# A weight ring of seven 1 MB pairs in place of thirteen 512 KB tiles, in a two-block transformer kernel

## The chip, the core and the metric

The kernel runs on one core of one Trainium2 chip. The metric is the device time of one launch in microseconds. A core has a matrix engine (TensorE, in the profile PE, with its weight load as PEld), three engines for elementwise work (VectorE as DVE, ScalarE as ACT, GpSimd as POOL), a queueing engine (SyncE, as SP) and 16 DMA engines that all queues share. SP issues the weight transfers, POOL the gathers, and ACT a few small transfers. Everything is float32.

## The reference, cut to what matters

Two transformer blocks are run on 256 tokens of width 1024. The first has two attentions and a layer that looks up 16 experts for each of 8 heads and each token; the second has a spatial mixer, an attention over blocks and a dense layer of width 4096.

```python
def first_block(x, c, ...):
    mod = silu(c) @ w_ada + b_ada                      # 6 vectors of 1024
    h = modulate(rms_norm(x, g_mix), sh1, sc1)
    proj = h @ w_in                                    # q, k, v of both attentions, two gates
    o_sb, o_d = stick_breaking_attention(...), dilated_attention(...)
    merged = sigmoid(gate_sb) * (o_sb @ w_sb_o) + sigmoid(gate_d) * (o_d @ w_dil_o)
    x = x + gt1 * (merged @ w_out)
    h2 = modulate(rms_norm(x, g_ffn), sh2, sc2)
    return rms_norm(x + gt2 * peer_ffn(h2, w_pq, peer_keys, peer_u, peer_v), g_final)

def peer_ffn(h, ...):                                  # per token: 8 heads x 16 experts
    q = h @ w_pq
    expert, gate = top 16 of the sums of two top 16 lists of q against peer_keys
    act = gelu(h . peer_u[expert])
    return sum(gate * act * peer_v[expert])            # u and v rows: 2 x 1024 numbers each

def second_block(x, p, ...):
    u, v, q, k, v_att, g_a, g_b = split(rms_norm(x) @ w_in_2)
    x = x + (sigmoid(g_a) * sgu_mixer(u, v) + sigmoid(g_b) * moba_attention(q, k, v_att)) @ w_out_2
    x = x + square(relu(rms_norm(x) @ w_ff1_2)) @ w_ff2_2
    x = x + sigmoid(rms_norm(x) @ w_ple_gate_2) * (p @ w_ple_proj_2)
    return rms_norm(x)
```

## The kernel before, in words

**Tiles and stages.** The 256 tokens are two tiles of 128. First come the projections of the first block (w_in, in part for both tiles), then the branches and the output projection of tile 0. From then on the expert rows of tile 0 are gathered (128 turns; the names call one head of one tile a unit u, so u is 0 to 15, and each unit has 16 turns k), while TensorE does the attentions, gates, branches and output of tile 1 beside them (`beside`). Then the rows of tile 1 are gathered (128 more turns) while TensorE runs the whole second block of tile 0. Last, the second block of tile 1 runs with no gathers beside it.

**A gather turn.** POOL issues one indirect DMA (L1289) that brings 128 rows of 8 KB, 1 MB, into a row slot. There are nine row slots of 1 MB: three of their own, two in the buffers `tmp` and `merged` (only for the first 62 rows), and four that are the ring's slots 0 to 7, two each. VectorE takes the dot products (L2181), ScalarE and VectorE make the weight (L1417, L2201, L2209), ScalarE writes a diagonal matrix into `dg` (L1425, sixteen in turn) and TensorE multiplies it with the second half of the row (L757 to L760, `accumulate`), two turns behind. The last of these counts `v_used`, which frees the row slot for POOL and the diagonal for ScalarE.

**Weights.** All weights but w_ada come in tiles of 512 KB, 4 KB in each of 128 partitions (384 KB for the branches), in the order of the list FIRST. The tile names: sq, sk, sv, dq, dk, dv are the projections of the two attentions, ga and gb the gates, br0 and out0 the branches and output of tile 0 (lsv, ldv, lga, lgb, br1, out1 those of tile 1), q0 to q15 the query weights of the 16 units in two halves, w0 and w1 the 138 tiles of the second block for tile 0 and tile 1. SP goes through FIRST in order (`first_tiles`, L1206). Each tile waits until TensorE has used what was in its slot. The ring has 13 slots: 12 in rotation at first; while the row slots hold slots 0 to 7, only 5; near the end of the gathers the eight come back. Six tiles of tile 1 (`GUESTS`) go early into the unused row slots. The modulation weights w_ada come first in 512 KB blocks on SP (L1224) and then as eight 2 MB transfers on POOL's queue (L1271), two buffers in turn, each freed by the dot products L1918 on VectorE.

**Turns and weights together.** During the second block of tile 0, one step is one weight tile (`quarter`, L968, four matmuls of 128x512) and one gather turn. The two halves of a unit's query (`query`, L718) run in turns 5 and 7 of every 16; in FIRST they stand two to three tiles apart. The wait of a tile on TensorE is in `tile`:

```python
slot, landed = SLOT[name]
pe.wait_ge(tile_in[slot], landed)
```

## Time and profile before

| | |
|---|---|
| time, median of 3 runs | 1377.2 us (1374.71 to 1377.25) |
| the profiled execution: time, span of its trace | 1375.88 us, 1374.1 us |
| TensorE busy, VectorE busy | 1199.9 us, 735.0 us |
| ScalarE busy, GpSimd busy | 334.5 us, 304.4 us |
| DMA traffic | 517.51 MB, 106557 packets, mean 377 GB/s |
| GpSimd's queue (gathers, large part of w_ada) | 285.23 MB, 51.0% of 16 engines' span |
| SyncE's queue | 227.25 MB, 43.6% |
| chain of work that ended last | TensorE 54%, DMA 32%, VectorE 8%, ScalarE 3% |

All times in the trace count from the start of its span. "A <- B" in a view means that A writes from B, and in the waits that A waited for B. A matmul group of the page shows modelled ends, so a busy TensorE is not one at its peak. PEclk is the granted share of TensorE's clock. The DMA share of a stretch can read slightly over 1, since packets overlap; at 1.00 to 1.03 the DMA engines have no gap. Packets of a row of a gather are 8 KB, packets of a weight tile 4 KB, and each transfer adds 16 packets of a few bytes.

### The profile page before, as it was taken

To read this page: it belongs to the slowest core of one execution; us is meant where nothing else is said; L and a number is where in the kernel's file an instruction comes from. 1 tells how busy PE (TensorE), PEld (TensorE's weight loads), DVE (VectorE), ACT (ScalarE), POOL (GpSimd) and SP (SyncE) were. 2 spreads that over 40 slices of the span, in tenths; PEclk is the share of its full clock that TensorE was granted. 3 is DMA by queue.
4 is the path that set the end of the run, shared out by engine and by line. 5 is a ranking of instruction groups with operands and counts; after the bars stand their busy time and mean duration, and the time that the engine had idled before them with its cause. 6 is when DMAs were issued, how large, how long until landed. Compare 5 with 4: busy or idle time off the path is not lost.

```text
span 1374.1 us, 17081 instructions
## 1 busy us (share of the span) xinstructions
PE 1199.9 (87%) x6004; PEld 615.1 (45%) x6004; DVE 735.0 (53%) x2087; ACT 334.5 (24%) x914; POOL 304.4 (22%) x271
## 2 busy tenths in 40 slices
PE   5999998978867866779898989899877999999998
PEld 4788975535534531223333333333222344544444
DVE  6456467967776776886556565554644332310002
ACT  2412134222211231333222211211110243311102
POOL 0000013434333343343232322222233100000000
PEclk9999999989898998789999999999999999999999
DMA  9999989999999999999999999999999899778882
GB/s 370 405 363 395 384 328 370 419 419 418 417 417 418 412 407 419 409 367 415 416 417 416 415 412 416 401 417 411 417 417 417 313 411 363 224 265 285 291 302 87
DMA packets 106557, 517.51 MB, mean 377 GB/s; under 512 B 12133, under 2 KB 12901, under 8 KB 73194
## 3 DMA queue, kind: packets, MB, share of 16 engines
q0 software_dynamic: 41088, 285.23, 51.0%
q1 hardware_dynamic: 63364, 227.25, 43.6%
q10 hardware_dynamic: 2022, 3.95, 0.8%
q8 instruction: 49, 0.80, 0.2%
q14 instruction: 34, 0.28, 0.1%
HBM read 513.76 MB, written 1.05 MB: 375 GB/s over the span
## 4 chain that ended last, share of the span: by engine, by line
PE 54%; DMA 32%; DVE 8%; ACT 3%; issue 2%; SPq 1%; POOL 0%; ACTq 0%; DVEq 0%
PE ps_M L968 28%; DMA ring<-in_w_second 15%; DMA ring<-in_peer_uv,arena 12%; PE ps_T L757 8%; PE ps_M L489 3%; DMA ring<-in_w_pq 2%; DMA arena<-in_w_ada 2%; PE ps_M L512 2%; PE ps_M L659 2%; DVE ring L2181 2%; PE ps_M L682 2%; PE ps_OT L956 1%; PE ps_M L718 1%; DVE arena L2181 1%; DVE arena L1918 1%
## 5 line engine op out<-in xcount | busy, mean ns | idle before, releaser
L968 PE MATMUL ps_M<-ring,arena 128*128 128x512 f32 x1072 | 499.0, 604 | 36.2 <-DMA ring<-in_w_second 35.3
L968 PEld LDWEIGHTS ps_M<-ring,arena 128*128 128x128 f32 x1072 | 190.7, 190 | 300.2 <-issue 242.3
L1289 POOL DMA_INDIRECT ring<-in_peer_uv,arena x137 | 160.3, 1170 | 336.0 <-PE ps_T L760 317.9
L757 PE MATMUL ps_T<-ring,arena 64*64 64x512 f32 x274 | 159.5, 671 | 58.0 <-ACT arena L1425 58.0
L1289 POOL DMA_INDIRECT arena<-in_peer_uv,arena x105 | 121.4, 1156 | 234.6 <-PE ps_T L760 221.1
L758 PE MATMUL ps_T<-ring,arena 64*64 64x512 f32 x274 | 159.5, 671 | 0.0
L759 PE MATMUL ps_T<-ring,arena 64*64 64x512 f32 x274 | 159.5, 671 | 0.0
L760 PE MATMUL ps_T<-ring,arena 64*64 64x512 f32 x274 | 159.5, 671 | 0.0
L757 PE MATMUL ps_T<-arena 64*64 64x512 f32 x210 | 115.7, 635 | 22.1 <-ACT arena L1425 22.0
L1417 ACT ACTIVATE arena<-arena 128x2 f32<-128x2 f32 x128 | 25.8, 201 | 393.3 <-DVE arena L2201 389.9
L2181 DVE SCALAR_TENSOR_TENSOR ring<-ring,merged 128x1024 f32<-128x1024 f32 x73 | 88.8, 1220 | 53.1 <-DMA ring<-in_peer_uv,arena 52.8
L760 PE MATMUL ps_T<-arena 64*64 64x512 f32 x210 | 115.8, 635 | 0.0
L759 PE MATMUL ps_T<-arena 64*64 64x512 f32 x210 | 115.8, 635 | 0.0
L758 PE MATMUL ps_T<-arena 64*64 64x512 f32 x210 | 115.7, 635 | 0.0
L2181 DVE SCALAR_TENSOR_TENSOR ring<-ring,arena 128x1024 f32<-128x1024 f32 x64 | 77.9, 1220 | 35.2 <-DMA ring<-in_peer_uv,arena 32.7
L757 PEld LDWEIGHTS ps_T<-ring,arena 64*64 64x64 f32 x274 | 29.3, 141 | 142.9 <-ACT arena L1425 92.3
L2181 DVE SCALAR_TENSOR_TENSOR arena<-arena,merged 128x1024 f32<-128x1024 f32 x55 | 67.1, 1222 | 34.7 <-DMA arena<-in_peer_uv,arena 34.7
L1425 ACT ACTIVATE arena<-ident,arena 128x64 f32<-128x64 f32 x256 | 80.8, 340 | 19.8 <-DVE arena L2209 16.9
L2181 DVE SCALAR_TENSOR_TENSOR arena<-arena 128x1024 f32<-128x1024 f32 x50 | 60.8, 1220 | 19.7 <-DMA arena<-in_peer_uv,arena 16.1
L659 PEld LDWEIGHTS ps_M<-hT,ring 128*128 128x128 f32 x512 | 62.9, 203 | 13.2 <-issue 13.1
L659 PE MATMUL ps_M<-hT,ring 128*128 128x128 f32 x512 | 66.4, 290 | 0.0
L2209 DVE SCALAR_TENSOR_TENSOR arena<-arena 128x2 f32<-128x2 f32 x128 | 20.5, 160 | 79.1 <-ACT arena L1417 77.4
(349 smaller groups left out, 1727.3 us busy)
## 6 DMA issues: line engine op xcount, KB each, us to landing
ring<-in_w_second SPq DMA_DIRECT2D x274, 512.0 KB, 4.7
ring<-in_w_in SPq DMA_DIRECT2D x66, 512.0 KB, 13.1
arena<-in_w_ada POOLq DMA_DIRECT2D x8, 2048.0 KB, 16.2
ring<-in_w_pq SPq DMA_DIRECT2D x28, 512.0 KB, 5.3
arena<-in_w_ada SPq DMA_DIRECT2D x16, 512.0 KB, 15.1
ring<-in_w_out SPq DMA_DIRECT2D x16, 512.0 KB, 5.5
ring<-in_w_br SPq DMA_DIRECT2D x16, 384.0 KB, 9.4
ring<-in_peer_uv,arena POOLq DMA_INDIRECT x137
```

Of the source, the lines that this page charges most:

```text
L489: m = mm(bank[:, 0:T], w[:, c, :], hT[:, c, :], start=c == 0, stop=c == KC - 1)
L512: m = mm(bank[:, 0:n * P], hT[:, c, tile_tok(tt)], slots(lo, n)[:, :, c, :], start=c == 0, stop=c == KC - 1)
L659: m = mm(bank[:, 0:P], w[:, c, :], hT[:, c, tile_tok(t)], start=c == 0, stop=c == KC - 1)
L682: m = mm(bank[:, 0:P], w[:, c, :], tile_merged[:, c, :], start=c == 0, stop=c == KC - 1)
L757: mm(ps["T0"][low, :], d[low, :], row[low, 0:512], start=first, stop=last)
L758: mm(ps["T1"][low, :], d[high, :], row[high, 512:1024], start=first, stop=last)
L759: top = mm(ps["T0"][high, :], d[low, :], row[low, 512:1024], start=first, stop=last)
L760: bottom = mm(ps["T1"][high, :], d[high, :], row[high, 0:512], start=first, stop=last)
L968: m = mm(bank, left[c], w[:, c, :], start=first and c == 0, stop=last and c == 1)
L1289: pool.indirect_dma_start(row_slots[s], None, A["peer_uv"], bass.IndirectOffsetOnAxis(ap=expert[:, u % 3, k:k + 1], axis=0))\
L1425: F(dg[:, n % 16, :], twice, ACT.Copy, scale=wgt[:, u % 2, k:k + 1]).then_inc(diag_ready, 1)
L2181: V.scalar_tensor_tensor(up_row(n), up_row(n), 1.0, h_rows[u // NH], ALU.mult, ALU.mult, accum_out=act_x[:, u % 2, k:k + 1]).then_inc(dott ...
```

## The change

The ring has 14 slots and is handled as seven pairs. Two neighbours in FIRST are one transfer of 1 MB (8 KB in each partition; 6 KB for two branch tiles), with one semaphore and one wait for a free pair. `in_pairs` lays the weights out so on the host. The number of bytes is the same. In the opening all 14 slots rotate. While rows hold slots 0 to 7, three pairs rotate in place of five tiles. The nine row slots stay as they were.

The extra 4 KB per partition is taken from the arena: `dg` has 8 diagonals in place of 16 (ScalarE waits for `v_used` of 8 turns back, not 16), half of the table `rel0` moves into `tmp`, `expert_f` and `act_t` share room with `pos_f` and `act_b`.

FIRST is rearranged where two neighbours were not neighbours before: the halves of a query stand together. TensorE's instructions and their order are the same. SP has 203 fewer transfers and one more (rel0 comes in two).

```diff
-RING, OPENING = 13, 12
+RING = 14
-ARENA = 28272
-SECOND_END = 18254
+ARENA = 27248
+SECOND_END = 17792
+DIAGONALS = 8
...
     if phase in (3, 4):
-        FIRST += [(what, c) for c in range(3)] + [(f"q{u}", 0), (what, 3), (f"q{u}", 1)] + [(what, c) for c in range(4, KC)]
+        FIRST += [(what, c) for c in range(4)] + [(f"q{u}", 0), (f"q{u}", 1)] + [(what, c) for c in range(4, KC)]
...
-for n in range(LEAD + QUARTERS):
+for n in range(0, LEAD + QUARTERS, 2):
+    turns_here = [t for t in TURN_AT[n:n + 2] if t is not None]
+    for t in turns_here:
+        if t // TOPK + NH + 2 < NU and t % TOPK == 5:
+            FIRST += [(f"q{t // TOPK + NH + 2}", half) for half in (0, 1)]
     if n >= LEAD:
-        FIRST.append(("w0", n - LEAD))
-    if TURN_AT[n] is not None:
-        if TURNS // TOPK + NH + 2 < NU and TURNS % TOPK in (5, 7):
-            FIRST.append((f"q{TURNS // TOPK + NH + 2}", TURNS % TOPK // 7))
+        FIRST += [("w0", n - LEAD), ("w0", n - LEAD + 1)]
...
-order = list(range(OPENING))
-for n, name in enumerate(FIRST):
+order = list(range(PAIRS))
+for n in range(0, len(FIRST), 2):
+    pair = FIRST[n:n + 2]
     if n == SHARED:
-        order = [RING - 1] + list(range(VR, RING - 1))
+        order = [6, 4, 5]
...
-        rel0 = carve(AH, P)
+        rel0 = tmp[:, 4:8, :].rearrange("p a (h k) -> p (a h) k", k=P), carve(AH // 2, P)
...
             def tile(name):
                 slot, landed = SLOT[name]
-                pe.wait_ge(tile_in[slot], landed)
+                pe.wait_ge(tile_in[slot // 2], landed)
...
-                for name in FIRST[lo:hi]:
+                for name in FIRST[lo:hi:2]:
...
-                    to = slots(slot, 1).rearrange("p s c n -> p (s c n)")[:, 0:n]
-                    eng.dma_start(to, src).then_inc(tile_in[slot], 16)
+                    to = slots(slot, 2).rearrange("p s c n -> p (s c n)")[:, 0:n]
+                    eng.dma_start(to, src).then_inc(tile_in[slot // 2], 16)
...
-                if n >= 16:
-                    act.wait_ge(v_used, n - 15)
-                F(dg[:, n % 16, :], twice, ACT.Copy, scale=wgt[:, u % 2, k:k + 1]).then_inc(diag_ready, 1)
+                if n >= DIAGONALS:
+                    act.wait_ge(v_used, n - DIAGONALS + 1)
+                F(dg[:, n % DIAGONALS, :], twice, ACT.Copy, scale=wgt[:, u % 2, k:k + 1]).then_inc(diag_ready, 1)
...
+def in_pairs(tiles, order=None):
+
+
+    tiles = tiles[list(range(len(tiles))) if order is None else order]
+    return tiles.reshape(len(tiles) // 2, 2, P, -1).transpose(0, 2, 1, 3).reshape(len(tiles) // 2, P, -1)
```

Two places of SP's order are shown. SP's queue where the gathers begin, before: after the output tiles of tile 0 (in_w_out) come q0 (in_w_pq), the guests (to the arena), lsv and the first gates of tile 1 (in_w_in), and q2 (in_w_pq) with the next three gates. M0 and M1 are the PSUM banks whose finished product frees the slot.

```order
L1206 DMA ring<-in_w_pq 128x1024 [waits done_M1]
L1206 DMA arena<-in_w_in 128x1024 [waits ada_used] x4
L1206 DMA arena<-in_w_pq 128x1024 [waits ada_used] x2
L1206 DMA ring<-in_w_in 128x1024 [waits done_M0]
L1206 DMA ring<-in_w_in 128x1024 [waits done_M1]
L1206 DMA ring<-in_w_in 128x1024 [waits done_M0]
L1206 DMA ring<-in_w_in 128x1024 [waits done_M1]
L1206 DMA ring<-in_w_in 128x1024 [waits done_M0]
L1206 DMA ring<-in_w_in 128x1024 [waits done_M1]
L1206 DMA ring<-in_w_pq 128x1024
L1206 DMA ring<-in_w_pq 128x1024 [waits done_M0]
L1206 DMA ring<-in_w_in 128x1024 [waits done_M1]
```

The same place of SP's queue in the change: the row after q2 is the pair (lga1, lgb1).

```order
L1216 DMA ring<-in_w_pq 128x2048 [waits done_M1]
L1216 DMA arena<-in_w_in 128x2048 [waits ada_used] x2
L1216 DMA arena<-in_w_pq 128x2048 [waits ada_used]
L1216 DMA ring<-in_w_in 128x2048 [waits done_M1] x3
L1216 DMA ring<-in_w_pq 128x2048 [waits done_M1]
L1216 DMA ring<-in_w_in 128x2048 [waits done_M1]
L1216 DMA ring<-in_w_in 128x2048 [waits done_M0]
```

What moved: before, the three tiles lga1, lgb1 and lga2 waited only for output tiles of tile 0 (slots 9 to 11). Now pair 4, where lga1 and lgb1 go, holds lsv0 and lsv1 and is free only after TensorE's `values(("lsvA", 1))`, and lga2 and lgb2 wait for `values(("lsvB", 1))`.

SP's queue at unit 11 of the second block's weights, before: w_pq is q11, SA the bank of the queries.

```order
L1206 DMA ring<-in_w_second 128x1024 [waits done_M0]
L1206 DMA ring<-in_w_second 128x1024 [waits w_used] x2
L1206 DMA ring<-in_w_pq 128x1024 [waits w_used]
L1206 DMA ring<-in_w_second 128x1024 [waits done_M1]
L1206 DMA ring<-in_w_second 128x1024 [waits w_used]
L1206 DMA ring<-in_w_pq 128x1024 [waits w_used]
L1206 DMA ring<-in_w_second 128x1024 [waits w_used]
L1206 DMA ring<-in_w_second 128x1024 [waits done_SA]
```

The same place in the change:

```order
L1216 DMA ring<-in_w_second 128x2048 [waits done_M0]
L1216 DMA ring<-in_w_pq 128x2048 [waits w_used]
L1216 DMA ring<-in_w_second 128x2048 [waits done_M1]
L1216 DMA ring<-in_w_second 128x2048 [waits w_used]
L1216 DMA ring<-in_w_second 128x2048 [waits done_SA]
L1216 DMA ring<-in_w_second 128x2048 [waits done_M0]
```

What moved: q11 stands as one pair ahead of w0 14 and 15, and the pair w0 18 and 19 waits for the second half of the query (`done_SA`, turn 7); before, the tile that followed the first half's slot was w0 18 as well, but it waited for the first half alone (turn 5). All SP transfers behind it wait in the same queue. This recurs at units 12 to 15.

## Rows read from the trace of the kernel before

**Rows 1.** busy us of PE, PEld, DVE, ACT, POOL, then PEclk, DMA share, GB/s

```profile
34.00:172.00 138.00, 135.94 (x849) 117.10 (x848) 75.34 (x152) 36.54 (x77) 6.18 (x8) 1.00 1.02 387
...
206.00:240.00 34.00, 29.42 (x211) 18.70 (x213) 24.94 (x74) 14.54 (x33) 13.78 (x12) 1.00 0.97 370
240.00:578.00 338.00, 259.96 (x1762) 140.76 (x1754) 249.57 (x772) 82.36 (x283) 128.82 (x111) 0.89 1.01 416
...
612.00:1068.00 456.00, 402.06 (x1804) 147.41 (x1796) 251.94 (x762) 94.90 (x306) 132.15 (x114) 1.00 1.02 414
...
1104.00:1374.00 270.00, 262.81 (x857) 127.08 (x855) 46.97 (x93) 61.07 (x122) 0.00 (x0) 0.99 0.79 276
```

**Rows 2.** chain of waits, 976 to 995: start us, us, what

```profile
976.04 16.81 DMA ring<-in_w_second
...
992.99 1.97 PE ps_M L968 x4
```

**Rows 3.** waits from 612 to 1068: us in total, times, longest us

```profile
PE ps_M L968 <- DMA ring<-in_w_second: 35.1, 44, 1.9
...
PE ps_SA L718 <- DMA ring<-in_w_pq: 17.4, 9, 2.6
```

**Rows 4.** DMA queues, 267 to 269: packets, MB, share of 16 engines

```profile
q0 software_dynamic: 76, 0.52, 63.3%
q1 hardware_dynamic: 76, 0.31, 38.5%
```

**Rows 5.** DMA queues, 139 to 147 (w_ada beside branch tiles)

```profile
q0 software_dynamic: 474, 1.94, 60.5%
q1 hardware_dynamic: 466, 1.27, 41.5%
```

**Rows 6.** DMA totals of 10:38 (4 KB packets alone)

```profile
DMA packets 3155, 11.49 MB, mean 410 GB/s; under 512 B 350, under 2 KB 350, under 8 KB 3155
```

**Rows 7.** DMA totals of 252:256 (gathers alone)

```profile
DMA packets 228, 1.65 MB, mean 414 GB/s; under 512 B 27, under 2 KB 27, under 8 KB 27
```

**Rows 8.** DMA totals and SP's queue, 238 to 476

```profile
DMA packets 16288, 99.41 MB, mean 418 GB/s; under 512 B 1812, under 2 KB 1812, under 8 KB 6262
...
q1 hardware_dynamic: 5010, 17.18, 18.0%
```

**Rows 9.** DMA totals and SP's queue, 646 to 782

```profile
DMA packets 10638, 56.57 MB, mean 416 GB/s; under 512 B 1183, under 2 KB 1183, under 8 KB 6292
...
q1 hardware_dynamic: 5750, 20.92, 38.2%
```

**Rows 10.** busy us of 872:888, columns as in Rows 1

```profile
872.00:888.00 16.00, 16.00 (x64) 5.77 (x63) 6.23 (x20) 3.84 (x12) 4.23 (x4) 1.00 0.99 382
```

**Rows 11.** chain of waits, 134 to 158

```profile
134.96 14.94 DMA arena<-in_w_ada
...
149.99 4.68 DVE arena L1918 x8
```

**Rows 12.** TensorE after the last w_ada: start us, us, what, idle before

```profile
155.37 1.16 PE L670 MATMUL ps_M<-arena,ring 128*128 128x128 f32 x8 [0.93 <-DVE arena L2034]
```

**Rows 13.** SP's issues of branch tiles in order of time

```profile
130.21 14.76 SPq L1206 DMA_DIRECT2D ring<-in_w_br  x8
```

**Rows 14.** TensorE at a query of the second DMA stage

```profile
867.52 2.02 PE L718 MATMUL ps_SA<-hT,ring 128*128 128x128 f32 x16 [1.88 <-DMA ring<-in_w_pq]
...
876.11 1.98 PE L968 MATMUL ps_M<-ring,arena 128*128 128x512 f32 x4
...
879.04 1.98 PE L968 MATMUL ps_M<-ring,arena 128*128 128x512 f32 x4
```

**Rows 15.** GpSimd's gathers in order of time

```profile
206.04 0.94 POOL L1289 DMA_INDIRECT ring<-in_peer_uv,arena  x1 [3.37 <-PE ps_M L512]
```

**Rows 16.** TensorE where the gathers end

```profile
1080.96 1.98 PE L968 MATMUL ps_M<-ring,arena 128*128 128x512 f32 x4 [0.70 <-DMA ring<-in_w_second]
```

**Rows 17.** the page's DMA issues, KB each, us to landing

```profile
ring<-in_w_second SPq DMA_DIRECT2D x274, 512.0 KB, 4.7
```

More of the change, by code:

```diff
@@ L139 @@
 LATE = ALONE - 12
+PAIRS = RING // 2
 KEPT = {("q8", half): ("q7", half) for half in (0, 1)}
 SLOT, BEFORE = {}, {}
-loads, held = [0] * (RING + len(GUESTS)), [None] * RING
-order = list(range(OPENING))
-for n, name in enumerate(FIRST):
+loads, held = [0] * (PAIRS + len(GUESTS) // 2), [None] * PAIRS
+order = list(range(PAIRS))
+for n in range(0, len(FIRST), 2):
+    pair = FIRST[n:n + 2]
     if n == SHARED:
-        order = [RING - 1] + list(range(VR, RING - 1))
+        order = [6, 4, 5]
     elif n == LATE:
-        by_last_row = sorted(range(VR // 2), key=lambda s: landings[OWN + LENT + s][-1])
-        order = [2 * s + i for s in by_last_row for i in (0, 1)] + order
-    if name in KEPT:
-        SLOT[name] = SLOT[KEPT[name]]
-        order.append(SLOT[name][0])
-        continue
-    if name in GUESTS:
-        s = RING + GUESTS.index(name)
-        loads[s] += 1
-        SLOT[name] = (s, 16)
-        continue
-    if name == ("lga", 0):
-        order = [0, 1]
-    s = order.pop(0)
-    if name not in KEPT.values():
-        order.append(s)
-    loads[s] += 1
-    SLOT[name] = (s, 16 * loads[s])
-    BEFORE[name] = held[s]
-    held[s] = name
+        order = sorted(range(VR // 2), key=lambda s: landings[OWN + LENT + s][-1]) + order
+    if pair[0] in KEPT:
+        p = SLOT[KEPT[pair[0]]][0] // 2
+        order.append(p)
+    elif pair[0] in GUESTS:
+        p = PAIRS + GUESTS.index(pair[0]) // 2
+        loads[p] += 1
+    else:
+        if pair[0] == ("lga", 0):
+            order = [0]
+        p = order.pop(0)
+        if pair[0] not in KEPT.values():
+            order.append(p)
+        loads[p] += 1
+        BEFORE[pair[0]] = held[p]
+        held[p] = pair[1]
+    for i, name in enumerate(pair):
+        SLOT[name] = (2 * p + i, 16 * loads[p])
 (X3_SQ, X3_ROOT, R3, X4_SQ, X4_ROOT, R4, R4H, LN_PART, _, LN_SUM, LN_NEG, LN_SQ, LN_ROOT, LN_INV, X5_SQ, _, X5_SUM, R5,
@@ L373, in build @@
         quarter_done = {}
-        tile_in = [sem(f"tile_in{s}") for s in range(RING + len(GUESTS))]
+        tile_in = [sem(f"tile_in{s}") for s in range(PAIRS + len(GUESTS) // 2)]
         vec_in, ident_in, x_in, key_in, const_in, const2_in = (
@@ L480, in tile @@
                 slot, landed = SLOT[name]
-                pe.wait_ge(tile_in[slot], landed)
+                pe.wait_ge(tile_in[slot // 2], landed)
+                if name[0] in ("br0", "br1"):
+                    both = slots(slot // 2 * 2, 2).rearrange("p s c n -> p (s c n)")
+                    return both[:, slot % 2 * 6 * P:(slot % 2 + 1) * 6 * P].rearrange("p (c n) -> p c n", n=P)
                 return slots(slot, 1)[:, 0]
@@ L1247, in _ @@
             eng.dma_start(pT[:, :, :].rearrange("p a b -> p (a b)"), A["p_2"]).then_inc(tables_in, 16)
-            eng.dma_start(rel0.rearrange("p a b -> p (a b)"), A["rel0"]).then_inc(tables_in, 16)
+            for half in range(2):
+                eng.dma_start(rel0[half].rearrange("p a b -> p (a b)"), A["rel0"][:, half * 8 * P:(half + 1) * 8 * P])\
+                    .then_inc(tables_in, 16)
             eng.dma_start(bsT, A["b_sgu_spatial_2"]).then_inc(tables_in, 16)
@@ L1265, in _ @@
             slot, landed = SLOT[STICKS[-1]]
-            pool.wait_ge(tile_in[slot], landed)
+            pool.wait_ge(tile_in[slot // 2], landed)
             pool.wait_ge(first_in[1][KC - 1], 16)
```

52 lines of the change are left out of this document (29 added, 23 removed).

## The prediction, made before the result was known

> **What bounds the kernel now.** I read the busy table by stage first [rows 1]. Four stages differ. From 34 to 172 TensorE is busy for 135.94 of 138 us: the projections bound it, and DMA is full beside it. From 240 to 578 and from 612 to 1068 the DMA engines have no gap (share 1.01 and 1.02), at 416 and 414 GB/s, while TensorE has one: expert rows and weights come as fast as the chip brings them, and bytes over rate is the time. From 1104 on TensorE is busy for 262.81 of 270 us and DMA at 0.79: weights are no bound there. The chain of waits in the second DMA stage [rows 2] alternates: 16.81 us from the issue of a weight tile to its landing, 1.97 us of matmuls that use it. That is the loop of a ring slot: five tiles in 18.95 us, one step (one tile of 0.52 MB, one gather of 1.05 MB) in about 3.8 us, which is 1.57 MB at 414 GB/s. TensorE does wait for weights in this stage, 35.1 us for w_second and 17.4 us for w_pq [rows 3], but since DMA has no gap meanwhile, this is where the shortage of bytes is felt and not its cause. So the change can save in four ways only: a higher rate, fewer holes in the DMA stages, fewer bytes in them, or an earlier start of them.
>
> **How the queues share.** With both queues busy, 76 packets of the gathers and 76 of the weights move in 2 us [rows 4]: one for one, whatever their size, so 8 KB stands against 4 KB, and the weights get 0.31 of 0.83 MB. In the stretch with w_ada (4 KB) beside branch tiles (3 KB) it is 474 to 466 [rows 5]. With pairs a weight packet is 8 KB (6 KB for branches): the weights get one half beside gathers and two thirds beside w_ada.
> The Trainium skill (DMA: Bandwidth & Descriptors, in "SWDGE vs HWDGE vs iDMA") puts the boundary at which an engine switches at 4096 B preferably. By that, queues would share bytes evenly and the change would alter no share; the trace disagrees, with 0.52 to 0.31 MB for equal counts.
>
> **1. Rate of the DMA stages.** In 238:476 the weights' queue has 17.18 of 99.41 MB (17%), and 417.7 GB/s are moved (99.41 MB in 238 us) [rows 8]; in 646:782 it has 20.92 of 56.57 MB (37%), and 416.0 GB/s [rows 9]. Neither has holes of size. The step of 1.7 GB/s over 20 points of small packets, carried on to none, gives +3.3 GB/s for the second stage (0.8% of 456 us, 3.6 us) and +1.5 GB/s for the first (0.37% of 338 us, 1.2 us): 4.8 us together, the halved count of completion packets in it. The lower end: 4 KB packets alone run at 410 GB/s [rows 6], gathers alone at 414 [rows 7], 1% per byte. 1% of 37% of 456 us and of 17% of 338 us is 1.7 + 0.6 = 2.3 us. The second pair is from short stretches, the first mixes other things; I take the middle, **-3.5 us**.
>
> **2. Holes in the second DMA stage.** It moves 414 GB/s as a whole [rows 1] and 416.0 in a stretch without holes [rows 9]: 0.48% of 456 us is 2.2 us of holes. One lies at 872:888, at 382 GB/s [rows 10]; just ahead TensorE waited for w_pq (1.88 us at 867.52) and then made steps of 2.93 us (876.11 to 879.04) [rows 14]. While TensorE stands, gathered rows fill their slots and no new gather is issued. With half of the bandwidth, a weight transfer lands sooner, and this wait is shorter. But the new order has a worse place, five times (units 11 to 15): the pair that takes the slots of a query is issued only when turn 7 has used its second half, and the quarter that needs it is one step away (three times) or none. Its landing: 1.05 MB at half of 418 GB/s is 5.0 us, and 3.4 us fixed (4.7 us for a tile [rows 17] less 1.3 us for its bytes at 410 GB/s), 8.4 us. TensorE waits 5.5 to 8.4 us there. What covers it: of seven row slots some three are in use by the dot products and the two turns that TensorE runs behind, so about four rows, 4.2 MB or 10 us of work at 418 GB/s, are still to land, and the weights queued behind them. DMA goes on. TensorE then gains 3.8 - 2.93 = 0.85 us per step and has some 14 steps until the next, 12 us. I take **-1.5 us**, with 0 and -2.2 as ends.
>
> **3. What is loaded ahead.** Before, lga1, lgb1 and lga2 (1.57 MB) land before the gathers get dense; in the change their pairs wait for lsv on TensorE. The gather at 206.04 waited for the same product (3.37 us, L512) [rows 15], so the pairs are issued at about 206 and 209. 1.57 MB at 418 GB/s is 3.8 us if DMA is full then. It is not: 206:240 moves 370 GB/s [rows 1], room for 34 x 48 = 1.63 MB. If every hole is hit, it costs nothing. The gathers that compete there are delayed a little, and VectorE takes rows as they land, so I take a third, **+1.3 us** (0 to 3.8). The two gathers in slots that held lsv no longer wait for it, but the turns that need them come later: nothing.
>
> **4. The end of the gathers.** The first pair that goes into a freed row slot must land whole; at 1080.96 TensorE already waited 0.70 us for its first tile [rows 16]. Another 0.52 MB at 418 GB/s is 1.25 us; shared half and half it also comes faster: **+0.7 us** (0 to 1.3). The last stage is bound by TensorE, with fourteen slots in place of thirteen: nothing.
>
> **5. The opening.** Eight tiles (4.2 MB, 10.2 us at 410 GB/s) lie ahead of the w_ada blocks that start TensorE; 1% of it is **-0.1 us**.
>
> **6. The last w_ada transfer.** It is on the path with no slack: issued at 134.96, 14.94 us to landing, then the dot products (4.68 us) on VectorE, and L2034 behind them in its queue, which frees TensorE's bank [rows 11]; TensorE stood 0.93 us for it at 155.37 [rows 12]. What it competes with is the weights' queue. Before, that queue is backlogged there and takes half. In the change pairs are issued as TensorE frees them. The branch tiles followed each other at 14.76 / 8 = 1.8 us [rows 13], so a branch pair (0.79 MB) comes every 3.7 us, 213 GB/s; with 6 KB against 4 KB it drains at three fifths of 405 GB/s, 243. So the queue runs dry between pairs, and there w_ada has everything. The bytes that land before its end are much the same, and so I take **0** (ends -0.9, what TensorE stood, and +6.9, below).
>
> **7. Nothing:** the diagonals (the cover: a turn's row can only land when the turn seven, at first nine, before it has given its slot back, so ScalarE's new wait for eight turns back is nearly always met; without that cover ScalarE would stand a step of 3.8 us, with the gates of TensorE's other work queued behind it); rel0 in two transfers behind the same wait; the shared rooms, whose writers are followed in order; TensorE's order, which is the same.
>
> **Sum.** -3.5 - 1.5 + 1.3 + 0.7 - 0.1 + 0 = -3.1 us. The profiled execution took 1375.88 us, of it 1374.1 us span; it becomes 1372.8 us. The runs of before (1374.71 to 1377.25) have a mean of 1376.4, 0.5 us over the profiled one, so I predict **1373.3 us**.
>
> **The rivals.**
> *All gains, no costs:* terms 1 and 2 at their ends, 3 and 4 at nothing, and the last w_ada 0.9 us sooner: -8.0 us, 1368.4. For it: holes enough at 206:240. Against: two short stretches must be read at their best.
> *The gain is used up:* the rate by the lower end (-2.3), new waits at the queries as large as the old ones (0), the late gates at 2.5 and the end at 0.7: +0.9 us, 1377.3. For it: 8 KB packets are barely better in rows 6 and 7.
> *The last w_ada is late (slower):* if the weights' queue is not drained between 139 and 149, w_ada gets a third of the bytes (4 KB against 8) and not 242 GB/s (1.94 MB in 8 us [rows 5]). 2.1 MB at a third of 405 is 15.5 us and not 8.7: +6.9 us, all on the path; against branch pairs (6 KB) alone it is +4.3. Sum +3.8 us, 1380.2. It decides from the point where more than about one pair is queued when this transfer starts. For it: in rows 5 the weights' queue is full. Against: it then had half, and now has more than TensorE's pace.
> *The queries' pair starves DMA:* if only two rows are outstanding when TensorE stops, 5 us of cover stand against 8.4, and 3 us are lost at five places: -3.1 + 1.5 + 15 = +13 us, 1390.
> *The fixed part of a transfer counts:* if a pair's landing sets the pace, TensorE's waits for weights (35.1 + 17.4 us [rows 3]) go, 1323.8. Against: DMA share 1.02 and 410 GB/s with 512 KB transfers back to back [rows 6].
> The Trainium skill (DMA: Bandwidth & Descriptors, "Rules for kernel authors") asks for 1 MiB or more per DMA, and "Bandwidth" gives 78% of peak at 1 MB and less below. By its fit of 2.0 us fixed per DMA an estimate would be 2 us saved for each of some 65 pairs. The trace disagrees: 410 GB/s at 512 KB.
>
> **How the numbers follow.** The forecast 0.42, all gains 0.13, gain used up 0.22, w_ada late 0.15, DMA starved 0.06, fixed part 0.02. A measurement of this kernel can tell about 0.2% (2.75 us) from no change. Faster by more: 0.32 of the forecast's 0.42 (3.1 is just over it, and its terms 1 to 3 move it by 2), 0.13 and 0.02: 0.47. Within: 0.10 and 0.20: 0.30. Slower: 0.02, 0.15 and 0.06: 0.23. The range reaches from all gains to w_ada late: 1367.5 to 1380.5.
>
> **What would show it.** Term 1: 418 to 419 GB/s in 646:782 with weights' packets at 8 KB, and equal counts of both queues where both are busy. Term 2: about 416 to 418 GB/s over 612:1068, TensorE's waits for w_second fewer but longer, five of them 5 to 8 us behind a query; holes there would prove the fourth rival. Term 3: the start of the full DMA stage with 206:240 above 400 GB/s. Term 4: the wait at the end at 1.5 to 2 us. Term 6: the last w_ada landing within 1 us of 149.9; at 154 the third rival holds. If the first DMA stage begins late though w_ada landed on time, term 3 is wrong. If both stages run at 414 to 416 as before, term 1 is.

## The result, and the profile after

The changed kernel takes **1397.94 us** (median; 1397.73 to 1400.0), the kernel before 1376.41 us in the same comparison. The ratio is 1.0156, interval 1.014 to 1.0172: 21.5 us slower, where 1373.3 us was predicted. The profiled execution took 1397.84 us, span 1396.0 us; the mean granted clock of TensorE is 0.939 (before 0.963).

Busy time by stage in the changed kernel, columns and stages as in [rows 1]:

```profile
34.00:172.00 138.00, 131.29 (x786) 111.66 (x785) 72.61 (x144) 35.23 (x73) 6.17 (x8) 0.98 0.98 374
...
206.00:240.00 34.00, 32.21 (x221) 22.91 (x220) 28.05 (x87) 13.32 (x31) 11.11 (x11) 1.00 1.01 411
240.00:578.00 338.00, 257.44 (x1751) 139.16 (x1754) 247.16 (x765) 84.87 (x282) 130.48 (x112) 0.88 1.01 415
...
612.00:1068.00 456.00, 406.69 (x1789) 153.99 (x1788) 247.36 (x753) 96.61 (x304) 125.00 (x112) 0.95 0.98 397
...
1104.00:1374.00 270.00, 268.54 (x880) 125.63 (x873) 49.90 (x97) 60.36 (x123) 0.00 (x0) 1.00 0.81 297
```

Two rows moved. In 34:172 TensorE is busy 131.29 us in place of 135.94: it stands 4.65 us longer. In 612:1068 the DMA engines move 397 GB/s in place of 414 at a share of 0.98. The start times of the 256 gathers, numbered from 0 here and below, put numbers to it. The first starts at 197.1 us (before 190.4: **+6.7 us**). From number 12 to number 132, the first DMA stage, it is 363.6 us (363.5: nothing). From number 132 to number 252 it is 484.1 us (469.4: **+14.7 us**). These two make 21.4 of the 21.5 us.

**The opening.** The chain of waits of the changed kernel (start us, us, what):

```profile
49.72 36.84 DMA arena<-in_w_ada
...
86.59 4.68 DVE arena L1930 x8
...
91.49 0.69 DVE tmp L2005
92.18 0.61 DVE tmp L2008
...
93.98 9.46 PE ps_M L498 x32
```

The second w_ada transfer takes 36.84 us and lands at 86.57; before, issued at 50.16, it landed at 76.75. VectorE's dot products with it (L1930) stand in its queue ahead of the rotation of a projection (L2005, L2008); TensorE waits 5.5 us for what ScalarE (L1321) passes on behind them. The DMA queues of 56:58 say why (packets, MB, share of 16 engines):

```profile
q1 hardware_dynamic: 78, 0.52, 63.6%
q0 software_dynamic: 76, 0.31, 38.4%
```

The counts are equal and the bytes are not: w_ada (q0) gets 0.31 MB in 2 us. Before, in the same 2 us, it had 107 packets and 0.44 MB against 112 and 0.39.

**The second DMA stage.** Around the second half of a query, the chain (736 to 764):

```profile
746.25 1.80 PE ps_SA L727 x16
...
748.06 7.88 DMA ring<-in_w_second
...
755.99 3.78 PE ps_M L977 x4
759.77 1.04 PE ps_T L766
...
761.33 1.91 PE ps_M L977 x4
```

TensorE ends the query (L727) at 748.05. That frees the slot, SP asks for the next quarters 0.01 us later, they land after 7.88 us, and TensorE has waited for them. GpSimd's gathers in order of time show what the DMA engines had meanwhile:

```profile
735.98 0.94 POOL L1301 DMA_INDIRECT arena<-in_peer_uv,arena  x1 [3.67 <-PE ps_T L769]
740.70 1.26 POOL L1301 DMA_INDIRECT arena<-in_peer_uv,arena  x1 [3.78 <-PE ps_T L769]
745.51 1.34 POOL L1301 DMA_INDIRECT ring<-in_peer_uv,arena  x1 [3.55 <-issue]
749.36 0.94 POOL L1301 DMA_INDIRECT ring<-in_peer_uv,arena  x1 [2.50 <-PE ps_T L769]
761.64 0.94 POOL L1301 DMA_INDIRECT ring<-in_peer_uv,arena  x1 [11.35 <-PE ps_T L769]
```

No gather is issued for 12.3 us, since TensorE frees no row. The four ahead of the gap landed at 747.4, 749.9, 753.0 and 760.4. The stretches of 740:750, 750:760 and 760:770 (columns as above):

```profile
740.00:750.00 10.00, 9.70 (x72) 5.18 (x68) 7.58 (x22) 4.02 (x17) 3.25 (x3) 1.00 0.94 364
750.00:760.00 10.00, 4.01 (x8) 1.47 (x12) 4.10 (x12) 0.20 (x1) 0.29 (x1) 0.70 0.98 398
760.00:770.00 10.00, 10.00 (x60) 4.00 (x53) 3.96 (x10) 5.51 (x19) 2.82 (x3) 0.96 0.80 316
```

The deepest hole in DMA (a stretch in which the engines move less than they could, here 316 GB/s) comes after TensorE's stop at this query, a shallower one (364) ahead of it. A late pair and a hole stand at all five queries of units 11 to 15, but not alike. TensorE waits 4.22, 6.29, 2.50, 4.06 and 2.10 us for the pair behind the second half, 19.2 of the 30.2 us that it waits for w_second in 612:1068 (the rest, 0.96 to 2.78 us each, is ahead of the queries). At unit 13 the hole is shallow (383 GB/s at its lowest in steps of 4 us); at units 14 and 15 it lies wholly ahead of that stop, which begins at 888.3 and 962.0:

```profile
880.00:884.00 4.00, 3.23 (x13) 1.47 (x14) 0.60 (x3) 0.95 (x5) 0.94 (x1) 0.57 0.43 178
884.00:888.00 4.00, 4.00 (x28) 2.53 (x26) 3.63 (x13) 0.84 (x4) 0.00 (x0) 1.00 0.78 262
...
952.00:956.00 4.00, 4.00 (x19) 1.56 (x18) 3.86 (x9) 0.60 (x1) 2.00 (x2) 1.00 0.78 264
```

My theory before the experiments was: the opening is lost to the sharing of packets, and the second DMA stage to the place of the queries' pair in the order. The rival to both was the coarse ring: seven pairs are too few places, wherever they are put and whatever their packets.

### The profile page after: what moved, and what is told of

Read it like the earlier page. It is cut to its first block, busy times and chain, and to the rows that moved or that the text cites. A ratio compares the mean times of both kernels' runs of the same rounds, so it can differ in the third digit from the quotient of the medians.

```text
span 1396.0 us, 16887 instructions
## 1 busy us (share of the span) xinstructions
PE 1222.8 (88%) x6004; PEld 623.8 (45%) x6004; DVE 734.7 (53%) x2087; ACT 333.8 (24%) x914; POOL 299.3 (21%) x271
## 3 DMA queue, kind: packets, MB, share of 16 engines
HBM read 513.76 MB, written 1.05 MB: 369 GB/s over the span
## 4 chain that ended last, share of the span: by engine, by line
PE 57%; DMA 28%; DVE 9%; ACT 3%; issue 2%; SPq 0%; POOL 0%; ACTq 0%; DVEq 0%; POOLq 0%
PE ps_M L977 30%; DMA ring<-in_peer_uv,arena 11%; PE ps_T L766 9%; DMA arena<-in_peer_uv,arena 6%; DMA ring<-in_w_second 6%; DMA arena<-in_w_ada 5%; PE ps_M L668 2%; DVE ring L2193 2%; PE ps_M L521 1%; PE ps_M L691 1%; PE ps_SA L727 1%; PE ps_M L498 1%; DVE arena L2193 1%; DVE arena L1930 1%; PE ps_OT L965 1%
## 5 line engine op out<-in xcount | busy, mean ns | idle before, releaser
L977 PE MATMUL ps_M<-ring,arena 128*128 128x512 f32 x1072 | 514.1, 619 | 32.6 <-DMA ring<-in_w_second 32.6
L977 PEld LDWEIGHTS ps_M<-ring,arena 128*128 128x128 f32 x1072 | 194.8, 194 | 298.9 <-issue 274.7
L1301 POOL DMA_INDIRECT ring<-in_peer_uv,arena x137 | 157.3, 1149 | 345.0 <-PE ps_T L769 334.2
L766 PE MATMUL ps_T<-ring,arena 64*64 64x512 f32 x274 | 164.7, 691 | 65.6 <-ACT arena L1437 65.5
L767 PE MATMUL ps_T<-ring,arena 64*64 64x512 f32 x274 | 164.7, 691 | 0.0
L768 PE MATMUL ps_T<-ring,arena 64*64 64x512 f32 x274 | 164.7, 690 | 0.0
L769 PE MATMUL ps_T<-ring,arena 64*64 64x512 f32 x274 | 164.7, 690 | 0.0
L766 PE MATMUL ps_T<-arena 64*64 64x512 f32 x210 | 120.2, 658 | 30.0 <-ACT arena L1437 29.9
L767 PE MATMUL ps_T<-arena 64*64 64x512 f32 x210 | 120.2, 658 | 0.0
L769 PE MATMUL ps_T<-arena 64*64 64x512 f32 x210 | 120.2, 658 | 0.0
L768 PE MATMUL ps_T<-arena 64*64 64x512 f32 x210 | 120.2, 658 | 0.0
```

The source lines that it names most:

```text
L766: mm(ps["T0"][low, :], d[low, :], row[low, 0:512], start=first, stop=last)
L767: mm(ps["T1"][low, :], d[high, :], row[high, 512:1024], start=first, stop=last)
L768: top = mm(ps["T0"][high, :], d[low, :], row[low, 512:1024], start=first, stop=last)
L769: bottom = mm(ps["T1"][high, :], d[high, :], row[high, 0:512], start=first, stop=last)
L977: m = mm(bank, left[c], w[:, c, :], start=first and c == 0, stop=last and c == 1)
L1301: pool.indirect_dma_start(row_slots[s], None, A["peer_uv"], bass.IndirectOffsetOnAxis(ap=expert[:, u % 3, k:k + 1], axis=0))\
```

## The experiments

"Later queries" below stands for the edit of the second one; it is the base of several others. Each ratio is against the kernel before on the same chip (its medians were 1376.4 to 1376.8 us).

**Only the opening in small packets.** The change, but the pairs ahead of the first query are moved as two transfers of 4 KB per partition (3 KB for branch tiles) on the same semaphore. The packets are small again, and these pairs take twice as many transfers.

```diff
+    if n < FIRST.index(("q0", 0)):
+        HALVED.add(pair[0])
...
-        loads[p] += 1
+        loads[p] += 2 if pair[0] in HALVED else 1
...
-                    eng.dma_start(to, src).then_inc(tile_in[slot // 2], 16)
+                    for lo, hi in ((0, n // 2), (n // 2, n)) if name in HALVED else ((0, n),):
+                        eng.dma_start(to[:, lo:hi], src[:, lo:hi]).then_inc(tile_in[slot // 2], 16)
```

> The change, with only the pairs ahead of the first query's weights (those of the opening) moved as two transfers of 4 KB per partition; later pairs keep 8 KB. Theory A: the opening gives back 6 to 7 us and nothing else moves, 1391 us, with the first gather at 190 to 191 and the stage 612:1068 at 397 GB/s as in the change. Theory B (the ring's coarseness): 1398 us, first gather at 197. A third possibility: TensorE, on time again in the opening, meets later pairs of 6 and 8 KB packets that slow the later w_ada transfers (the third rival of the prediction), and only 2 to 3 of the 6.7 us come back, 1395 us.

Measured: 1391.4 us (ratio 1.0095, 1.0064 to 1.0126; single runs 1382.6 to 1392.8), 6.5 us under the change. The first gather starts at 190.3, the w_ada transfer lands at 76.84, TensorE is busy 136.07 us in 34:172. The second DMA stage stays at 398 GB/s. So the opening is the work of the packets (with their transfers) and not of the ring, and it is separate from the rest.

**The queries' pair one place later.** For units 11 to 15 the pair of query weights is asked for behind the two quarters that it stood ahead of:

```diff
     turns_here = [t for t in TURN_AT[n:n + 2] if t is not None]
+    if n >= LEAD:
+        FIRST += [("w0", n - LEAD), ("w0", n - LEAD + 1)]
     for t in turns_here:
         if t // TOPK + NH + 2 < NU and t % TOPK == 5:
             FIRST += [(f"q{t // TOPK + NH + 2}", half) for half in (0, 1)]
-    if n >= LEAD:
-        FIRST += [("w0", n - LEAD), ("w0", n - LEAD + 1)]
```

> The change, with the pair of weights of queries 11 to 15 asked for one pair of quarters later, behind the two quarters that it stood ahead of, so that the quarters no longer queue behind a slot that TensorE frees last. Packets, ring and rooms as in the change. Theory A (the query's place in the order starves DMA five times): 612:1068 goes from 397 to about 412 to 418 GB/s, TensorE's waits of 6 us at L977 behind the query go, and 10 to 16 us come back: 1382 to 1388 us, with the first gather still at 197. Theory B (three pairs are too few places for the quarters in any order): the holes move and stay, 1395 to 1400 us. Theory C (the rest of the loss is the clock of TensorE, which fell because of the stalls): the granted clock in 612:1068 rises from 0.95 to 0.97 or more together with the rate.

Measured: **1377.16 us** (ratio 1.0012, 0.9997 to 1.0027), 20.8 us under the change, and 5 us better than I expected at best. Its stage 612:1068, and 740:750 to 760:770:

```profile
612.00:1068.00 456.00, 413.48 (x1846) 153.72 (x1846) 256.18 (x770) 96.58 (x312) 131.84 (x117) 0.98 1.01 418
...
740.00:750.00 10.00, 9.73 (x58) 4.58 (x59) 8.59 (x26) 3.58 (x15) 2.83 (x3) 1.00 1.01 420
750.00:760.00 10.00, 8.90 (x52) 3.80 (x50) 5.17 (x13) 4.47 (x18) 2.56 (x3) 1.00 1.01 419
760.00:770.00 10.00, 10.00 (x57) 3.68 (x56) 4.69 (x13) 3.24 (x8) 2.88 (x3) 1.00 1.01 420
```

No hole is left. The clock is back at 0.98, as theory C had it, but together with the waits, so this run doesn't tell the two apart. TensorE's waits for weights are all but gone (waits in 612:1068; before 35.1, [rows 3]):

```profile
PE ps_M L977 <- DMA ring<-in_w_second: 1.4, 2, 1.1
...
PE ps_T L766 <- ACT arena L1437: 38.1, 25, 4.1
```

The second row has grown: TensorE now waits for the diagonals that ScalarE writes, 38.1 us in all (18.7 in the change, 0.4 in the kernel before), and VectorE ahead of it waits 155 us for gathered rows (before 77). The shortage of bytes has passed from the weights to the rows; it has not gone.

From gather 132 to gather 252 it takes 463.1 us: 21.1 less than the change, 6.3 less than before. The DMA engines move 193 MB between the two gathers in either kernel, at 398 GB/s in the change and 417 here. The first gather starts at 196.3: the opening is untouched, and its loss is what stands between this and a gain.

**The kernel before, with both halves of a query asked for together.** Is it the place alone, or does it take the coarse ring as well?

```diff
-        if TURNS // TOPK + NH + 2 < NU and TURNS % TOPK in (5, 7):
-            FIRST.append((f"q{TURNS // TOPK + NH + 2}", TURNS % TOPK // 7))
+        if TURNS // TOPK + NH + 2 < NU and TURNS % TOPK == 5:
+            FIRST += [(f"q{TURNS // TOPK + NH + 2}", half) for half in (0, 1)]
```

> The kernel before, with its ring of 13 single slots, and one edit: both halves of the weights of queries 11 to 15 are asked for at turn 5, as the change does, not at turns 5 and 7. Theory A1 (this place in the order alone starves DMA): 612:1068 falls from 414 to 400 GB/s or less, 1388 us or more. Theory A2 (it takes the coarse ring as well: a pair waits for the later of two tiles, and a quarter behind it too): less than 5 us lost, 1377 to 1381 us.

Measured: 1394.57 us (ratio 1.0136, 1.0116 to 1.0155). This one edit costs the kernel before 18 us, with its single slots and its packets. Its row of 612:1068:

```profile
612.00:1068.00 456.00, 398.92 (x1764) 147.93 (x1764) 246.66 (x746) 93.04 (x299) 131.09 (x111) 0.97 0.99 398
```

The place alone (A1) is enough. SP stands here from 663.86 to 678.82 for a slot that a query's second half holds; in the change it is 664.61 to 681.81. The hole opens towards the end of that wait, while TensorE is busy throughout:

```profile
675.00:680.00 5.00, 5.00 (x32) 3.11 (x31) 4.86 (x10) 1.34 (x4) 1.23 (x1) 1.00 0.79 275
```

So a hole needs no stop of TensorE behind the second half. TensorE does stop once per query, for 3.9 to 4.5 us, but ahead of the second half (664.85 to 669.24), for the tile that now stands behind both halves in the order.

**Both repairs together.**

> The change with both repairs: the opening's pairs as two transfers of 4 KB per partition, and the pair of the weights of queries 11 to 15 one pair of quarters later. Two separate causes: the 6.5 us of the opening come off the run with the later queries (1377.2 us), 1370 to 1371 us, 0.4% faster than the kernel before; first gather at 190, 612:1068 at 418 GB/s. Rival: the last stage is bound by TensorE from about 1070 on and TensorE's own work is the limit further ahead too, so that a gather stage that starts sooner ends no sooner: 1374 to 1377 us.

Measured: **1372.51 us** (1370.56 to 1375.03), ratio 0.9967, 0.9953 to 0.998: 4.3 us faster than the kernel before, the only version here that is. Against later queries alone it is 4.65 us, of the opening's 6.5. So it lies 1.5 us above what I expected, and below the rival's range. The second DMA stage runs at 418 GB/s:

```profile
612.00:1068.00 456.00, 411.53 (x1848) 153.51 (x1848) 254.89 (x767) 94.47 (x309) 131.45 (x117) 0.99 1.01 418
```

**The queries' pair two places later**, on top of both repairs (the pair is kept back for one more round of the loop).

```diff
-TURNS = 0
+TURNS, OWED = 0, []
...
+    FIRST += OWED
-    for t in turns_here:
-        if t // TOPK + NH + 2 < NU and t % TOPK == 5:
-            FIRST += [(f"q{t // TOPK + NH + 2}", half) for half in (0, 1)]
+    OWED = [(f"q{t // TOPK + NH + 2}", half) for t in turns_here if t // TOPK + NH + 2 < NU and t % TOPK == 5 for half in (0, 1)]
```

> The run with both repairs, and the pair of the queries' weights yet one pair of quarters later (two behind its place in the change). If one place was enough and the pair still lands ahead of its use, nothing changes: 1372.5 us within 0.2%. If the place matters on both sides, the weights of a query are now late themselves: TensorE waits for in_w_pq at L729 five times by several us, DMA gets holes there, 1380 us or more.

Measured: 1383.82 us (ratio 1.0053, 1.0035 to 1.007), 11.3 us over both repairs. The waits of 612:1068 now have

```profile
PE ps_SA L728 <- DMA ring<-in_w_pq: 22.7, 5, 6.6
```

five waits for the query's own weights, one at each unit. One pair too early costs 21 us, one too late 11: the window is one place wide.

**All pairs in small packets**, first in the change as it is. The edit is that of the first experiment, with its condition taken away:

```diff
-    if n < FIRST.index(("q0", 0)):
+    if True:
         HALVED.add(pair[0])
```

> The change, with every pair moved as two transfers of 512 KB and 4 KB per partition on one semaphore. Ring, rooms, order and waits stay those of the change; only the packets are small again. Theory A (packet size acts on the sharing of the DMA engines): the opening gives back its 6.7 us (first gather at 190 to 191, the w_ada transfer issued at 49.72 lands near 77 instead of 86.6), the DMA stages fall from 420 back to about 417 GB/s (0.7% of 794 us, 5.5 us lost), and the stalls behind the queries stay, a little longer. Sum about 1398 - 7 + 5 = 1396 us. Theory B (the coarse ring itself, fewer places in which a weight can be asked for, makes both losses): nothing in the opening changes, 1398 + 5 = 1403 us. Theory C (everything is the packets): back to 1376 us.

Measured: 1439.41 us (ratio 1.0459, 1.0419 to 1.05), outside all three expectations. The opening is right again (first gather 190.4), but the second DMA stage falls to 358 GB/s. I had taken the large packets for a gain of 1% there, and they are worth 48 us against the version with small packets in the opening alone. Is this only the stall behind a query, made longer?

**The same with later queries.**

> Every pair as two transfers of 4 KB per partition, and the queries' pair one place later: the ring of pairs without large packets. With 4 KB everywhere and the queries where they stood the run took 1439 us, 42 us more than with 8 KB. Theory A (the stall behind a query is the whole of that: half the bandwidth beside the gathers' 8 KB becomes a third, the late pair lands later, and the stall of one query delays the next): with the order mended both the 42 us and the 21 us go, 1375 to 1379 us, 612:1068 at 414 to 416 GB/s (against 418 with 8 KB). Theory B (weights in 4 KB packets are too slow in general for a ring of seven pairs): 1390 us or more, with holes spread over 612:1068.

Measured: 1415.96 us (ratio 1.0279, 1.0259 to 1.0298): theory B. Against both repairs, where only the opening is in small packets, the small packets of the later pairs, in twice as many transfers, cost **43.5 us**. The DMA queues of 700:702 in this kernel, and its DMA issues in 612:1068 (xcount, KB each, median us from issue to landing):

```profile
q0 software_dynamic: 74, 0.57, 68.0%
q1 hardware_dynamic: 72, 0.27, 33.0%
```
```profile
ring<-in_w_second SPq DMA_DIRECT2D x114, 512.0 KB, 12.6
ring<-in_w_pq SPq DMA_DIRECT2D x10, 512.0 KB, 14.1
ring<-in_peer_uv,arena POOLq DMA_INDIRECT x62, 10.6
```

and the same of both repairs:

```profile
ring<-in_w_second SPq DMA_DIRECT2D x61, 1024.0 KB, 9.6
ring<-in_w_pq SPq DMA_DIRECT2D x5, 1024.0 KB, 9.1
ring<-in_peer_uv,arena POOLq DMA_INDIRECT x66, 18.4
```

With 4 KB against 8 KB the weights get 0.27 MB in 2 us, 135 GB/s. What TensorE uses is one tile of 0.52 MB in 3.8 us, 138 GB/s. The share is the demand, with nothing over to make good a late pair; 1 MB takes 7.8 us by it, and its second half lands up to 18 us after its issue. A third of the engines was enough for the kernel before, whose slots are asked for one by one; that this is why it could live on it is read from the shares, and was not tried by itself. The doubled number of transfers was not taken apart from the packet size either; the kernel before has as many (442 transfers on SP's queue against 443) and loses nothing by them. With 8 KB the weights' share can reach one half, a pair lands 9 to 10 us after its issue, and the waiting passes to the gathers, whose queue is long (18.4 us from issue to landing, 4.7 steps, against 10.6 here). The chain of this kernel still has the queries in it:

```profile
655.76 18.11 DMA ring<-in_w_pq
...
674.01 3.75 PE ps_SA L729 x16
```

**w_ada in rows of 16 KB**, to test the sharing from the other side. On later queries, with the opening's pairs at 8 KB, the array is laid out so that one partition's share of a 2 MB transfer is one row.

```diff
-        w_ada_v = A["w_ada"].rearrange("b p k -> p b k")
+        w_ada_v = A["w_ada"]
...
-    x["w_ada"] = x["w_ada"][0].T.reshape(6 * KC, P, D)
+    x["w_ada"] = x["w_ada"][0].T.reshape(6 * KC, P, D).transpose(1, 0, 2)
```

> The run with the later queries, and w_ada laid out so that one partition's share of a 2 MB transfer is one row of 16 KB in place of four of 4 KB; weight pairs keep 8 KB. If packets share one for one whatever their size, w_ada now takes two thirds beside the weights: the transfer issued at 49.7 lands at about 70 (86.6 in the change, 76.8 before), the last well ahead of 149, and the first gather comes at 190 or, if weights get late for TensorE instead, at 192 to 195; 1370 to 1374 us. Rival (a packet is cut at some smaller size, or the sharing is by bytes): w_ada as in the change, first gather at 196, 1377 us.

The queues of 56:58:

```profile
q0 software_dynamic: 33, 0.54, 63.6%
q1 hardware_dynamic: 37, 0.29, 35.3%
```

The transfer landed at 69.73, as expected (about 70). Packets of 16 KB and 8 KB are served one for one, like those of 8 and 4 KB. Yet the first gather still starts at 196.3, and the time is 1378.38 us (ratio 1.0009, 1.0 to 1.0018). So a third queue must be late. The chain:

```profile
69.10 12.69 DMA merged<-tmp
...
81.81 0.70 DVE tmp L2008
82.54 0.70 DVE arena L2011
...
83.70 7.19 PE ps_M L498 x32
```

These are the swaps of the rotation, transfers of 64 KB in small rows (1152 packets for 1.57 MB in 34:172, on a queue of their own). The last of the first group of four took 12.69 us, before 7.58. The chain has a second one further on, of 11.50 us. By the counts above, a transfer of few bytes in many packets waits its turns behind ever larger ones.

**w_ada in rows of 8 KB.** The ratio to the weights' packets is one again, as before, at twice the size (two blocks of the array in a row). The w_ada transfers on POOL's queue and the first blocks on SP's queue are read from the new layout to match:

```diff
-    x["w_ada"] = x["w_ada"][0].T.reshape(6 * KC, P, D)
+    x["w_ada"] = x["w_ada"][0].T.reshape(3 * KC, 2, P, D).transpose(0, 2, 1, 3).reshape(3 * KC, P, 2 * D)
```

> The run with the later queries, and w_ada laid out so that two of its blocks are one row of 8 KB; weight pairs keep 8 KB. The ratio of packets is 1 to 1 again, as before, but both are twice as large. If the ratio alone matters (packets counted one for one), the w_ada transfer issued at 49.7 lands at 76 to 77 as before, the first gather comes at 190 to 191, and the time is that of the run with both repairs, 1371 to 1373 us. If the size itself matters as well (the swaps of 64 KB in 1 to 2 KB rows wait behind larger packets; in the run with 16 KB rows one took 12.7 us, 7.6 before, and TensorE stood for it), the first gather comes at 192 to 195 and the time is 1374 to 1376 us.

Measured: 1378.28 us (ratio 1.0007, 0.9995 to 1.0019). The second w_ada transfer takes 25.0 us (before 26.6), as the ratio says, and lands at 76.78 (76.75 before) though it is issued 1.6 us later, at 51.78. But the swaps take up to 11.87 us, TensorE waits for them as with 16 KB rows, and the first gather starts at 198.3, 7.9 us later than before. The size matters too, and by more than I expected (192 to 195). Some 2 us of the 7.9 do not come from the swaps: the first blocks of w_ada land up to 1.5 us later than in the run with 16 KB rows, and TensorE comes to the same products (L521) at 52.45 and not 50.47.

```profile
79.09 11.87 DMA merged<-tmp
...
90.98 0.70 DVE tmp L2008
```

**Eight diagonals in the kernel before.**

```diff
-                d, row = dg[:, n % 16, :], down_row(n)
+                d, row = dg[:, n % 8, :], down_row(n)
...
-                if n >= 16:
-                    act.wait_ge(v_used, n - 15)
-                F(dg[:, n % 16, :], twice, ACT.Copy, scale=wgt[:, u % 2, k:k + 1]).then_inc(diag_ready, 1)
+                if n >= 8:
+                    act.wait_ge(v_used, n - 7)
+                F(dg[:, n % 8, :], twice, ACT.Copy, scale=wgt[:, u % 2, k:k + 1]).then_inc(diag_ready, 1)
```

> The kernel before with eight diagonals in place of sixteen (ScalarE's eighth diagonal back must have been used), nothing else of the change. My reading: the wait is nearly always met, 1376 us within 0.2%. Rival: ScalarE stands for it around the queries, TensorE gets its gates late, and part of the 13 us of the second DMA stage appears here: 1380 us or more, with waits of ScalarE for PE at L1425.

Measured: 1376.83 us (ratio 1.0001, 0.9991 to 1.0011), 414 GB/s in 612:1068. The eight diagonals cost the kernel before nothing, as the prediction's point 7 had it.

## Why the prediction was wrong, point by point

**The views were read rightly.** Both losses stood among the rivals. "The queries' pair starves DMA" is the second loss by its mechanism: two rows or fewer were still to land when each of the five late pairs could be asked for. Its price was 15 us for the five places; moving the pair gave back 21. "The last w_ada is late" has the right cause, the w_ada transfer's smaller share, at the wrong transfer, and that its price of +6.9 us lies so near the +6.7 us of the opening is luck. They had chances of 0.06 and 0.15, and it was not weighed that both could hold.

**The step that failed most** is in term 2: "about four rows, 4.2 MB or 10 us of work at 418 GB/s, are still to land, and the weights queued behind them. DMA goes on." Its neighbours held or were priced too high: the places were five, the pair's landing was priced at 8.4 us (4.9 to 8.1, here 7.88) and TensorE's wait at 5.5 to 8.4 us (6.29 here, 2.1 to 4.2 at the other four). The cover did not hold. When SP could ask, at 748.06, two rows were under way and one more followed (two at units 11 and 13, one at units 14 and 15); and no weights were queued, since the waiting pair holds up every pair behind it in SP's order. The last weights had landed at 739.15, 8.9 us earlier (7.4 to 13.6 at the other four). The DMA queues of 740:748:

```profile
DMA packets 411, 2.97 MB, mean 372 GB/s; under 512 B 49, under 2 KB 49, under 8 KB 49
...
q0 software_dynamic: 410, 2.96, 93.9%
```

Gathers alone, so each row took 2.5 us of the engines (1.05 MB at 414 GB/s [rows 7]) and not a step of 3.8: the cover was used up while TensorE was still working, ahead of its stop. I counted the cover from the moment at which TensorE stops, and with weights in the queue. TensorE misses them at 749.70 (755.99 less 6.29): the weights' queue had then been empty for 10.5 us. It could have been worked out from the order alone, since with three pairs in the ring the queue is empty as soon as one of them waits and the other two have landed.

What the prediction left out is the **clock**. After the 6.29 us the next group of matmuls took 3.78 us in place of 1.98, and from its start to the next group's start 5.34 us pass (755.99 to 761.33), before the stop 3.00 us (732.67 to 735.67). The granted clock of 750:760 is 0.70, a mean of its two levels (1.2 and 2.4 GHz). So this stop cost TensorE 2.3 us more than it waited. Behind the stops of 4.22 and 4.06 us the clock is at its lower level too (0.50 in 692:696 and in 892:896), behind that of 2.10 us it is not (1.00 in 964:968). How much of the 14.7 us is the clock's was not separated. The "0.85 us per step" by which TensorE was to catch up could not give back what the DMA engines had not moved: 397 GB/s and not the 418 of later queries, over 456 us, is 9.6 MB or some 23 us by my estimate.

**Term 5, the opening**, was costed by its bytes alone (-0.1 us). The paragraph on the queues had the rule, two thirds for the weights beside w_ada, and I used it at the last w_ada transfer only, where the chain [rows 11] had no slack. The slack of the second one, which lands in the middle of the projections, was not looked at: it now lands 9.8 us later, and VectorE waits 23.7 us in all for w_ada there (before 10.3). With five pairs and the 1 MB of peer_keys still to land at its issue, it is the backlog that the third rival asks for ("more than about one pair"), at another place.

**Term 6, the last w_ada**: right in itself. It takes 14.07 us (before 14.94) and is late, at 156.61, since all ahead of it is. The prediction's sign for the third rival (a landing at 154) was so met without its mechanism; the time from issue to landing would have told them apart:

```profile
142.54 14.07 DMA arena<-in_w_ada
```

**Term 1, the rate:** right for the second stage and understated: 420 GB/s in 646:782 with later queries (416 before [rows 9], 418 to 419 forecast), 418 over the stage. Its part for the first stage, 1.2 us or less, can't be seen: 363.5 us before, and 363.6, 364.3 and 362.2 us in the change, with later queries and with both repairs, while the kernel before with another order of its last queries, which leaves this stage alone, shows 361.5. 238:476 shows 419 to 420 GB/s against 418, and 476:578 is lower, 402 to 407 against 412. Why that stretch lost is not settled.

**Term 2's gain** was there once the order was mended: between gathers 132 and 252 it is 6.3 us less than before with later queries (2.4 in the profile with both repairs), where terms 1 and 2 have some 4 us for this stage.

**Term 3, what is loaded ahead** (+1.3 us): 206:240 runs at 411 GB/s, as its sign asked (above 400). From gather 0 to gather 12 it is 33.9 us, as before (34.0). It cost nothing measurable. Both repairs, and the kernel before with eight diagonals, show 36.6 us there, with a granted clock of 0.90 in 172:206 instead of 1.00; since the kernel before shows it too, it is not the change's.

**Term 4, the end of the gathers** (+0.7 us): too small. TensorE waits where [rows 16] had 0.70 us:

```profile
1100.98 2.64 PE L977 MATMUL ps_M<-ring,arena 128*128 128x512 f32 x4 [2.41 <-DMA ring<-in_w_second]
```

2.41 us in the change and 3.20 us with both repairs, with the clock lower behind it (2.64 and 3.67 us for the group, 1.98 before): +2.4 and +4.2 us in wait and group together. It is a likely reason why not all of the gain ahead of it reached the end; that was not tried by itself.

**The rival "the fixed part of a transfer counts"** fell as it should: with later queries TensorE's waits for weights are all but gone (1.4 us), its waits for the rows' diagonals have come in their place (38.1 us), and the stage still takes the time that its bytes take at 418 GB/s.

With the two causes taken out, the time is near the sum: 1372.5 us against 1373.3 forecast. Its parts are not: term 3 cost nothing, term 4 more than forecast, and this version moves the opening in small packets. That the total fits so well is in part luck. The two causes that it lacked had been called unlikely.

## What to carry to other kernels

When a transfer waits for a slot, count what is queued behind it and from when: the cover of the other queue runs from the moment at which this one falls empty, at the rate that one queue then has, and not from the stop of the engine that misses the data. When packets grow in one queue, go through every transfer that lands beside it, the small ones above all, since each gets its turns and not its bytes; and before giving a larger share up again, look for the place where it is what keeps a coarse ring going. Where a small order table decides, try the neighbouring places: here one place too early cost 21 us and one too late 11. A wait that vanishes is not yet a gain: look for what is waited for in its place.

## What the runs showed of the hardware

The DMA engines took the queues' packets one for one at every size tried: 76 to 78 with 4 and 8 KB, 33 to 37 with 16 and 8 KB, 74 to 72 with 8 and 4 KB. The Trainium skill (DMA: Bandwidth & Descriptors, "SWDGE vs HWDGE vs iDMA") puts the boundary at which an engine switches at 4096 B preferably; no run here agrees, up to 16 KB. A queue of 64 KB transfers in small packets took longer beside larger packets: in the first four groups, the last of four took 7.6 to 8.1 us beside packets of 4 KB, 10.2 to 11.9 beside 8 KB, and 9.4 to 12.7 beside 16 and 8 KB (in the change, beside 4 and 8 KB, 9.0 to 10.7 in the first three groups). Packet size did little for the rate itself, 414 to 418 GB/s over the second stage, and much for the time: 43.5 us between two kernels that differ in the packets of the weights behind the opening and in the number of their transfers. A wait of 6.3 us on TensorE was followed by matmuls at about half speed (3.78 us for a group of 1.98, granted clock 0.50 in 756:760).
